# Third weight block split early into a buffer of its own, last two rows of the wide phases bank by bank, and other engines adding more of the norm sums

## What is computed

```python
for i in range(DEPTH):                                     # first block, DEPTH = 2
    a_in = rms_norm(hs, norm_w[i, 0])
    mix = gated_deltanet(a_in, ...) if i == 0 else mlstm(a_in, ...)
    hs = hs + keep * rms_norm(mix, norm_w[i, 1])
    f = conv_ffn(rms_norm(hs, norm_w[i, 2]), ...)
    hs = hs + keep * rms_norm(f, norm_w[i, 3])
# second block, DEPTH = 2, with y = layer_norm(alpha * x + branch(x)):
#   layer 0: short convolution and sliding window attention (ev_in, ev_out), then swiglu (up2, down2)
#   layer 1: gated linear attention and latent attention (od_in, od_out), then swiglu (up3, down3)

def rms_norm(x, w):   y = xf * lax.rsqrt(jnp.mean(xf * xf, -1, keepdims=True) + RMS_EPS)
def layer_norm(x, g, b):   return (xf - mu) * lax.rsqrt(var + LN_EPS) * g + b
```

## Time and profile before

| | |
|---|---|
| median of 3 runs (lowest, highest) | 1443.23 us (1440.77, 1443.34) |
| the profiled execution's own time | 1440.93 us |
| its span | 1439.0 us |
| PE busy | 1416.4 us (98%), 11289 matmuls |
| DVE busy | 1010.7 us (70%) |
| ACT busy | 778.4 us (54%) |
| POOL busy | 295.1 us (21%) |
| chain that ended last | PE 79%, DVE 12%, ACT 4% |

### The profile page before, as it was taken

The page is one execution under the profiler, slowest core; times in us unless marked ns, Lnnn a source line. Parts: engine busy times, 40 slices in busy tenths (PEclk is TensorE's granted clock), DMA queues, the critical chain, the costliest instruction groups (busy, mean ns, idle before and its releaser), DMA issues.

```text
span 1439.0 us, 31650 instructions
## 1 busy us (share of the span) xinstructions
PE 1416.4 (98%) x11289; PEld 1358.5 (94%) x11289; DVE 1010.7 (70%) x1697; ACT 778.4 (54%) x1396; POOL 295.1 (21%) x348
## 2 busy tenths in 40 slices
PE   9999999999999999999999999999999999999997
PEld 8999888899999999999999999999999989999986
DVE  7884957659876476569888467687664697786645
ACT  6557324556655356456665356454454587654542
POOL 3804002103544000002454000013330003033300
PEclk9999999999999999999999999999999999999999
DMA  7551221244555536343665544446555433565552
GB/s 255 179 173 50 89 95 54 90 145 151 196 174 178 174 109 200 107 139 123 192 192 187 187 127 160 163 141 204 179 185 189 140 123 118 171 212 188 184 181 88
DMA packets 60852, 222.78 MB, mean 155 GB/s; under 512 B 6752, under 2 KB 6880, under 8 KB 60512
## 3 DMA queue, kind: packets, MB, share of 16 engines
q1 hardware_dynamic: 60480, 219.65, 47.6%
q10 hardware_dynamic: 288, 1.97, 0.4%
HBM read 220.54 MB, written 1.05 MB: 154 GB/s over the span
## 4 chain that ended last, share of the span: by engine, by line
PE 79%; DVE 12%; ACT 4%; issue 3%; DVEq 1%; DMA 0%; ACTq 0%
PE bank L438 20%; PE bank L439 20%; PE bank L440 20%; DVE wlo L413 3%; PE bank L459 2%; PE bank L1166 2%; PE bank L460 1%; PE bank L466 1%; DVE bank L945 1%; PE bank L3285 1%; PE bank L3286 1%; PE bank L3288 1%; ACT cv L829 1%; DVE cv L837 1%; DVE work L1780 1%
## 5 line engine op out<-in xcount | busy, mean ns | idle before, releaser
L413 DVE TENSOR_TENSOR wlo<-raw,whi 128x1024 fp32r<-128x1024 f32 x396 | 499.3, 1266 | 246.3 <-ACT whi L408 245.8
L408 ACT ACTIVATE whi<-raw 128x1024 fp32r<-128x1024 f32 x396 | 414.0, 1056 | 287.1 <-PE bank L440 241.7
L438 PE MATMUL bank<-xs,whi 128*128 128x258 f32 (+2 forms) x1976 | 566.7, 287 | 0.4 <-ACT big L2449 0.4
L439 PE MATMUL bank<-xs,whi 128*128 128x258 f32 (+2 forms) x1976 | 561.7, 284 | 0.0
L440 PE MATMUL bank<-xs,wlo 128*128 128x258 f32 (+2 forms) x1976 | 559.3, 283 | 0.0
L438 PEld LDWEIGHTS bank<-xs,whi 128*128 128x128 f32 x1976 | 372.7, 189 | 3.3 <-issue 1.2
L440 PEld LDWEIGHTS bank<-xs,wlo 128*128 128x128 f32 x1976 | 373.5, 189 | 0.0
L439 PEld LDWEIGHTS bank<-xs,whi 128*128 128x128 f32 x1976 | 372.8, 189 | 0.6 <-issue 0.2
L438 PE MATMUL bank<-hf,whi 128*128 (+3 forms) x848 | 241.2, 284 | 2.0 <-DVE cv L837 0.8
L439 PE MATMUL bank<-hf,whi 128*128 (+3 forms) x848 | 240.2, 283 | 0.0
L440 PE MATMUL bank<-hf,wlo 128*128 (+3 forms) x848 | 240.2, 283 | 0.0
(11 more groups left out here) (517 smaller groups left out, 1665.0 us busy)
## 6 DMA issues: line engine op xcount, KB each, us to landing
raw<-stream SPq DMA_DIRECT2D x411, 512.0 KB, 3.6
con<-consts SPq DMA_DIRECT2D x1, 1284.5 KB, 11.0
hs_sb<-hs SPq DMA_DIRECT2D x2, 544.0 KB, 4.3
work<-last ACTq DMA_DIRECT2D x1, 1024.0 KB, 8.8
y_out<-work SPq DMA_DIRECT2D x4, 256.0 KB, 2.0
big<-mla ACTq DMA_DIRECT2D x1, 896.0 KB, 7.0
par<-params SPq DMA_DIRECT2D x1, 420.0 KB, 8.3
par<-params SPq DMA_DIRECT2D x1, 224.0 KB, 5.0
```

Of the source, the lines that this page charges most:

```text
L408: nc.scalar.activation(whi[:, s, :], raw[:, s, :], ACT.Copy).then_inc(hi_split, 1)
L413: nc.vector.tensor_tensor(wlo[:, s, :], raw[:, s, :], whi[:, s, :].bitcast(F32), ALU.subtract).then_inc(block_split, 1)
L438: nc.tensor.matmul(out_, whi[:, slot, w], hi, start=start, stop=False)
L439: nc.tensor.matmul(out_, whi[:, slot, w], lo, start=False, stop=False)
```

## The change

Four edits, all around the seven transitions.

1. **The third block in a home of its own.** `third_hi` and `third_lo` split block n+2 into the buffer `cv` (seen as `cvr`), which needs no used slot of whi. `first_blocks_hi` and `first_blocks_lo` stand ahead of the norm and split n+2 first, then n, then n+1; the activation table is loaded between n and n+1. The split after the squares and the one before the mean are gone. The wave reads block n+2 from the new home. Three waits guard `cv`.
2. **The last two rows bank by bank.** `last_rows` gives each bank the parts of rows n-2 and n-1 of the phase (here n is the phase's count), six matmuls, before it goes to the next bank.
3. **post norms.** `FIRST_SUM` is 7: DVE adds squares 0 to 6, PE sums that and square 7.
4. **ln norms.** POOL adds y0 to y3 (`ln_pool`), DVE adds y4 to y6 after y5 and y6, PE sums those two and y7.

The core of the diff:

```diff
+    def third_hi(act, n):
+        act.wait_ge(block_loaded[n % SLOTS], 16 * (n // SLOTS + 1))
+        nc.scalar.activation(third_half(0), raw[:, n % SLOTS, :], ACT.Copy).then_inc(*S("third", "act").mark(f"hi{n}"))
+
+    def third_lo(dve, n):
+        dve.wait_ge(*S("third", "act").at(f"hi{n}"))
+        nc.vector.tensor_tensor(third_half(1), raw[:, n % SLOTS, :], third_half(0).bitcast(F32), ALU.subtract
+                                ).then_inc(*S("third", "dve").mark(f"lo{n}"))
+
+    def first_blocks_hi(act, phase, table=None):
+        n = used_after(phase)
+        third_hi(act, n + 2)
+        split_hi(act, n)
+        if table:
+            nc.scalar.preload_act_table_set(table)
+        split_hi(act, n + 1, count=2)
+
+    def first_blocks_lo(dve, phase):
+        n = used_after(phase)
+        third_lo(dve, n + 2)
+        split_lo(dve, n)
+        dve.wait_ge(*S("third", "dve").at(f"lo{n + 2}"))
+        split_lo(dve, n + 1, count=2)
...
+        def last_rows():
+            ks = (n - 2, n - 1)
+            for k in ks:
+                pe.wait_ge(block_split, splits(b0 + k))
+                ready(pe, k, None)
+            for m in range(8):
+                for k in ks:
+                    last = three(rhs_out(g0 + m, phase), (b0 + k) % SLOTS, m, hf[:, half[k], T], hf[:, half[n + k], T], False, k == n - 1)
...
-    FIRST_SUM, IN_BANK = 5, 5
+    FIRST_SUM, IN_BANK = 7, 5
...
-        sums_pe(pe, name, post_src(name), g, ((5, True, False), (6, False, False), (0, False, False), (7, False, True)), T1, POST_FIRST[name])
+        sums_pe(pe, name, post_src(name), g, ((0, True, False), (7, False, True)), T1, POST_FIRST[name])
...
-        split_hi(act, used_after(phase) + AHEAD - 1)
...
-        split()
...
+    POOL_SUM, DVE_SUM = 4, 7
...
+        for m in range(1, POOL_SUM):
+            pool.wait_ge(*S("norm", "dve").at(f"{name}_y{m}"))
+            if m > 1:
+                pool.wait_ge(*st.at(f"{name}_ysum{m - 1}"))
+            nc.gpsimd.tensor_tensor(total, yt(0) if m == 1 else total, yt(m), ALU.add).then_inc(*st.mark(f"{name}_ysum{m}"))
...
-        split_all(act, split_hi, "ml_out", 1, COUNT["ml_out"] - 2)
-        nc.scalar.preload_act_table_set(LN_EXP)
+        split_all(act, split_hi, "ml_out", 1, COUNT["ml_out"] - 4)
+        act.wait_ge(block_used, FIRST_BLOCK["ml_out"] + 1)
+        first_blocks_hi(act, "ml_out", LN_EXP)
```

More of the change, by code:

```diff
@@ L321, in build @@
     mix, mixr = shared("mix", [P, KC, T1], "mixr", [P, KC, T1])
-    cv = sb("cv", [P, 8, T1])
+    cv, cvr = shared("cv", [P, 8, T1], "cvr", [P, 8, T1])
     work = sb("work", [P, WORK])
@@ L454, in pe_tiles @@
                 for j in range(AHEAD):
-                    o, s = rhs_out(g0 + j, phase), (b0 + j) % SLOTS
+                    o, (high, low) = rhs_out(g0 + j, phase), home(j)
                     if k == 0:
-                        pe.wait_ge(block_split, splits(b0 + j))
+                        if j == AHEAD - 1:
+                            pe.wait_ge(*S("third", "dve").at(f"lo{b0 + j}"))
+                        else:
+                            pe.wait_ge(block_split, splits(b0 + j))
                         pe.wait_ge(bank_free, g0 + j + 1)
-                    mm(o, whi[:, s, w], xs[:, k, T], start=(k == 0), stop=False)
-                    mm(o, wlo[:, s, w], xs[:, k, T], start=False, stop=False)
+                    mm(o, high[:, w], xs[:, k, T], start=(k == 0), stop=False)
+                    mm(o, low[:, w], xs[:, k, T], start=False, stop=False)
             if k:
@@ L465, in pe_tiles @@
                 for j in range(AHEAD):
-                    last = mm(rhs_out(g0 + j, phase), whi[:, (b0 + j) % SLOTS, w], xs[:, KC + k - 1, T], start=False, stop=(k == KC))
+                    last = mm(rhs_out(g0 + j, phase), home(j)[0][:, w], xs[:, KC + k - 1, T], start=False, stop=(k == KC))
                     if k == KC:
@@ L536, in rows @@
                     bank_ready(pe, (g0 + m) % 8)
[L537 to L539 removed]
+                last = three(rhs_out(g0 + m, phase), (b0 + k) % SLOTS, m, hf[:, half[at] if i is None else at, T], hf[:, half[lo] if i is None else lo, T], k == 0, False)
             if done:
                 last.then_inc(block_used, 1)
+        def last_rows():
[6 more added lines that the diff above has]
+                    last = three(rhs_out(g0 + m, phase), (b0 + k) % SLOTS, m, hf[:, half[k], T], hf[:, half[n + k], T], False, k == n - 1)
+                    if m == 7:
+                        last.then_inc(block_used, 1)
+                if m < 7:
+                    last.then_inc(*S("wide", "pe").mark(f"{phase}_m{m}"))
         if n == 22:
@@ L547, in pe_wide @@
                     rows(k, i)
-            for k in range(17, 22):
+            for k in range(17, 20):
                 rows(k)
@@ L556, in pe_wide @@
                         between(pe, k)
-            for k in range(together, n):
+            for k in range(together, n - 2):
                 rows(k)
+        last_rows()
     def pe_sum(pe, name, g, src, T):
@@ L704, in post_act, with post_dve @@
         nc.scalar.activation(rs[:, 1, lo:T1], rs[:, 1, lo:T1], ACT.Exp, scale=-0.5).then_inc(*S("norm", "act").mark(f"{name}_scale"))
-    def post_dve(dve, name, g, row, split):
+    def post_dve(dve, name, g, row):
         v, lo = S("norm", "dve"), POST_FIRST[name]
@@ L2339, in ln_act, with ln_dve @@
         act_scale(act, name + "v", g + 1, rs[:, 0, 0:T2], T2, D, eps_ln, meanwhile=lambda: split_hi(act, fifth(phase)) if phase == "od_in" else None)
-    def ln_dve(dve, n, which, layer, phase, wide, split):
+    def ln_dve(dve, n, which, layer, phase, wide):
         name, g = f"ln{n}", G[f"lm{n}"]
@@ L3443, in _ @@
         gdn_mix_dve(dve)
-        split_all(dve, split_lo, "gdn_out", 1, COUNT["gdn_out"] - 2)
-        post_dve(dve, "post0", G["post0"], 1, lambda: split_lo(dve, used_after("gdn_out") + AHEAD - 1))
+        split_all(dve, split_lo, "gdn_out", 1, COUNT["gdn_out"] - 4)
+        first_blocks_lo(dve, "gdn_out")
+        post_dve(dve, "post0", G["post0"], 1)
         next_dve(dve, "post0", "pre1", 2, "up0")
         ffn_dve(dve, 0, G["up0"])
-        split_all(dve, split_lo, "down0", 1, COUNT["down0"] - 2)
-        post_dve(dve, "post1", G["post1"], 3, lambda: split_lo(dve, used_after("down0") + AHEAD - 1))
+        split_all(dve, split_lo, "down0", 1, COUNT["down0"] - 4)
+        first_blocks_lo(dve, "down0")
+        post_dve(dve, "post1", G["post1"], 3)
         next_dve(dve, "post1", "pre2", 4, "ml_in")
@@ L3452, in _ @@
         ml_dve(dve)
-        split_all(dve, split_lo, "ml_out", 1, COUNT["ml_out"] - 2)
-        post_dve(dve, "post2", G["post2"], 5, lambda: split_lo(dve, used_after("ml_out") + AHEAD - 1))
+        split_all(dve, split_lo, "ml_out", 1, COUNT["ml_out"] - 4)
+        first_blocks_lo(dve, "ml_out")
+        post_dve(dve, "post2", G["post2"], 5)
         next_dve(dve, "post2", "pre3", 6, "up1")
         ffn_dve(dve, 1, G["up1"])
-        split_all(dve, split_lo, "down1", 1, COUNT["down1"] - 2)
-        post_dve(dve, "post3", G["post3"], 7, lambda: split_lo(dve, used_after("down1") + AHEAD - 1))
+        split_all(dve, split_lo, "down1", 1, COUNT["down1"] - 4)
+        first_blocks_lo(dve, "down1")
+        post_dve(dve, "post3", G["post3"], 7)
         last_dve(dve, "post3", "b2")
```

92 lines of the change are left out of this document (57 added, 35 removed).

## The result

The changed kernel takes 1451.47 us (median of 6 runs, 1449.69 to 1454.74), the kernel before 1443.28 us beside it (6 runs, 1440.77 to 1443.94). The ratio is 1.0067, with a 95% interval of 1.0057 to 1.0077: **slower by 8.2 us** by the medians. In one later experiment, the one on ml_out and od_out alone, one of ten executions ran at a granted clock of 0.751 and took 1709.56 us; it is in that run's median of 1447.09, which is 1446.60 without it, and not in its ratio. The profiled execution of the changed kernel took 1449.69, span 1447.9, against 1440.93 and 1439.0.

A forecast was written before the change was run, and what follows sets the result against it. PE, busy 98% of the span, bounds the kernel, with room only in the seven transitions. Their terms, -0.6 -0.6 -0.15 +2.7 +0.45 -0.1 +2.3, sum to +4.0 us, given as 1447, range 1441 to 1451.5.

The forecast's parts named there:

- the sign: Whole kernel: slower by 4.0 us; chances slower 0.68, same 0.19, faster 0.13.
- The chain from L to C: ACT and DVE at the transitions: from n+2's load landing (L) to DVE free for the norm (C), 5.5 us.
- From C on, the layer norms: Layer norms, from DVE being free (C): y's, additions and PE's three summands, mean subtracted at C+5.1; bounds 4.85 and 6.3.
- E: Each transition's time zero: start of PE's first norm sum before the change, where the last row ends.
- The rival of 1.54 each: Layer norms: every POOL addition takes 1.54, adding 1.2 each, 1450.6; chance 0.24 together with the clock's fall.
- The landing L: n+2's load lands: gdn_out, down0 E-8.5; down1, down2 E-7.9; ev_out E-7.35; od_out E-5.5; ml_out E-5.1.
- The post norms: First scaled tile's shift: post0 and post1 -0.6 each, post3 -0.15, post2 +2.7.
- the clock: Rival in post2 and ln2: clock falls in PE's gaps, +3 to +5 together, 1450 to 1452; 0.24 with POOL's case.
- that row: Trace at the kernel's end: PE's clock was full for at least 3.2 us of idleness, then 1.2 GHz.
- the main case: Whole kernel: the forecast itself, slower by 2.5 to 6 us, chance 0.44.
- At nothing: Terms priced at zero: moved splits go into ACT's and DVE's idle time, hidden as long as the load is there.
- the load is there in time: Rival, all transitions: ACT isn't held at the third block; post norms -0.6, layer norms -1.3 each, 1436.9; chance 0.13.

The follow-up runs named there:

- the one on ml_out and od_out alone: Changed kernel with block n+2 split behind n and n+1 in ml_out and od_out only, ahead of them in the other five: 1447.09 us, ratio 1.0030.
- the run with the filled gap: Changed kernel plus 20 useless matmuls between last row and first norm sum in post2 and ln2 only: 1449.12 us, ratio 1.0051.
- the last version: Against the kernel before: own home, rows bank by bank, n+2 first behind the table load only in gdn_out and down0, sums chosen per place: 1437.84 us, ratio 0.9978.

## Why the prediction was right or wrong

**Right: the sign, the place and the mechanism.** ACT's split of n+2 waited in all seven transitions, for the load in six of the profiled ones, and the loss stood in ml_out and od_out, with the shape that the forecast gave: landing, three splits and the table, DVE, a gap on PE, a late first tile. Moving the table load into the wait, which shortens the chain and changes nothing else, took back 4.7 of the 7.0 in the transitions and left 0.09% in the total.

**The chain from L to C: nearly right.** Forecast 5.5, measured 5.66 in ml_out and in od_out. From C on, the layer norms were right: 5.1 forecast, 5.03 in ln0 (first y at E-1.41, mean at E+3.61) and in ln1. Inside that sum the terms were less good. GpSimd's three additions took 0.72 to 0.74 each, although VectorE's met them, and the chain ended at C+3.3 for 3.5; y7 ended at C+3.9 for 4.3. PE's three summands, which started 0.15 behind GpSimd's last addition and ran one after another, then set the mean. That the errors came to 0.1 is partly luck. The rival of 1.54 each didn't happen.

**The landing L: half right.** gdn_out, down0 and down1 were within 0.3 of the forecast; od_out was forecast at E-5.5 and measured at E-5.60; ml_out landed 0.7 earlier than forecast. ev_out landed 0.3 later (E-7.07 against E-7.35), which with 0.16 of the chain is the missing 0.4 of ln0. What I had not said is that L itself scatters: at down1 ACT started the split at E-7.85 in one profile and E-7.03 in another with the same code there, and where L is in the path each such tenth counts.

**The post norms: too small by 0.2 to 0.5 each.** I gave DVE 3.4 for the scaled bank and six additions. They took 0.41 and 3.16, and PE's first sum started at E+0.6 and E+0.7 in post0 and post1 where I had E+0.4, and at E+1.41 at down1 where I had E+0.9. That makes 0.2, 0.3 and 0.5 in three terms, 1.0 in the sum. In post2 the early landing outweighs it: 2.4 without the clock, for a forecast of 2.7.

**The step that failed: the clock was priced as a rival and not as part of the forecast.** I had written that PE would stand idle for 3.5 to 3.7 us in ml_out and od_out, and that 3.2 us of idleness had passed at the full clock in the earlier trace rows. I took that row as room and gave the fall 0.24 together with another case, so that the sum holds nothing for it. But my own forecast of the gap lay beyond the only length that the trace had shown at the full clock, so the fall belonged to the main case. (Nor was that length safe between matmuls: the clock fell after 1.84 to 2.36 us in other profiles.) It cost 0.62 in post2 (wave 2.10 instead of 1.48 after the tile) and 1.35 in ln2 (mean 2.92 after the first sum, 1.57 in ln0), 2.0 together; the run with the filled gap gave back 0.61 and 1.1, the latter being the 1.35 less a first sum that came 0.24 later. In numbers: 4.0, and 1.0 for three post norms, -0.3 for post2, 0.4 for ln0 and 2.0 for the clock make 7.1. By the end of down1 nearly all of post2's 0.62 was made up, so of the span the clock took about 1.4. As a rival I had priced the fall at 3 to 5 us, 1450 to 1452. The measured 1451.5 lies there, and at the very edge of my range, but not for that reason: the clock was less than half of the 4.2 by which I was short. The Trainium skill ("TensorE: Matmul & The Clock Gate", section "Why this matters for your kernels") advises against gaps of more than about 3 us; the trace agrees for the two gaps of 3.33, and the runs go further, with falls after 1.84 to 2.36.

**What stays open.** The medians differ by 8.2, the transitions of the profile by 7.0, so 1.2 is not accounted for; set against the span without the stretch near 120 us (8.9 less 2.6) it is 1.9. The granted clocks of the change's 6 runs read 0.993 to 0.995, those of the last version's 9 runs 0.996 to 0.999, and a profile with the stretch near 120 us alone reads 0.996 or 0.997; so every run of the change probably had two or more stretches, as its profile has three. Which ones the other runs had can't be read, since one execution is in the trace. The stretch near 120 us isn't part of the change's price as far as the runs show: it is in the profiles of five other versions, one of them no slower than before, and not in those of the kernel before and four others. Two profiles of versions near the change, the one with the gap filled and the one without GpSimd's additions, have one more such stretch at 1209 and 1180 us, with 1.9 us more between the wave of ln1 and the end of od_out than the change's. Whether runs of the change had it too, no profile shows.

**"At nothing" held only in part for the third split.** I said a moved split goes into idle time as long as the load is there. Placed first, with an early load and the table out of the way, it does: post0 and post1 of that run have the tile at E+2.65, for a forecast of E+2.6. Placed behind n and n+1 it stands 1.15 in DVE's path. The rival "the load is there in time" took the first case for all seven, 1436.9. The gains measured nearest to it are 0.5 in post0 and post1 and 0.8 in ln1, so an estimate from them for seven such places is -4.4 and not -6.3; in no run did the load of a layer norm land as early as the E-9 of that rival.

**Not seen at all: edits 1 and 2 depend on each other.** Rows that end together free two slots late. In the changed kernel the home hides that; alone it costs 0.95 in each layer norm.

## What to carry to other kernels

An in-order engine that waits for a load holds up all that stands behind it, so the order behind a wait is to be counted from the landing, and every instruction that doesn't need the load (here a table load of 1.28 us) belongs ahead of the wait. Before a piece of work is moved "into idle time", look where its engine's last piece ahead of the critical work starts: if that is paced by another engine, anything behind it is on the path. And if a forecast contains a new gap on PE between matmuls, the fall of the clock is a term of the sum with a chance of its own: at the transitions here it fell after eight of the ten gaps of 1.84 us and more. What it costs depends on what stands behind: 1.35 where six sum matmuls were in the path, almost nothing, once the next phases had run, between the tile and the wave of a post norm.

## What the runs showed of the hardware

- **Between rows and sums the fall shows behind the gap, not in it.** In the experiment on two phases PE is idle from 847 to 849 and reads 1.00 there and in 849 to 850, then 0.62 and 0.50. The useless matmuls behind the sum, which are there to keep the clock, come too late for that; 20 of them inside the gap kept it at 1.00.
- **The length of the gap does not decide alone.** At the transitions, over the profiles of the changed kernel and its variants, the clock fell after idle gaps of 1.84, 2.02, 2.08, 2.13, 2.36, twice 3.33 and 3.94 us, and did not after 1.55, 1.56, 1.76, 1.88 and 2.84, nor after any shorter one. Why, no run here tells.
- **What the clock puts between tile and wave of a post norm is made up.** At post2 the time from tile to wave was 2.10, 2.20 and 1.83 in the three profiles in which the clock fell there, and 1.48 or 1.49 in the others; the time from that wave to the next E was 0.5, 0.6 and 0.3 shorter than before in the three, and 0.1 longer in the others.
- **A table load holds ACT for 1.28 us and no more:** the next split starts 1.29 after it (646.57 to 647.86).
- **Additions of VectorE and GpSimd beside each other** (128x256): the one that started second was lengthened, and by little. VectorE's took 0.58 to 0.62 in place of 0.42 where it started 0.3 before the end of GpSimd's; GpSimd's took 0.84 to 0.86 in place of 0.73 where VectorE's had 0.26 to go (the last version); with 0.15 in common (ln1 with the table first) neither was lengthened. That is far less than what a split of 128x1024 did to GpSimd's product in the earlier trace rows, 1.54. GpSimd's additions, one on the other, start 0.86 to 0.89 apart.
